# Sums by adding transfers a round ahead, and split float32r passes, in a two-layer encoder kernel

## The reference

```python
def rmsnorm(x, g):
    xf = xf * lax.rsqrt(jnp.mean(xf * xf, axis=-1, keepdims=True) + EPS)
    return (xf * g.astype(jnp.float32)).astype(x.dtype)

def gla(h, w_in, w_gate, b_gate, norm_w, w_o):
    proj = h @ w_in                       # q, k, v, g and the low-rank ga (16 columns)
    gk = jax.nn.log_sigmoid((ga @ w_gate + b_gate).astype(jnp.float32)) / B_GATE_NORM
    ...

def conv_ffn(h, w_up, conv_w, conv_b, w_down):
    u = h @ w_up
    gate, up = u[..., :D_FF], u[..., D_FF:]          # D_FF = 2816
    gp = jnp.pad(gate, ((0, 0), (CONV_W - 1, 0), (0, 0)))
    conv = conv_b + conv_w[0] * gp[:, 0:S]
    for i in range(1, CONV_W):
        conv = conv + conv_w[i] * gp[:, i:i + S]
    return (jax.nn.silu(conv) * up) @ w_down
```

## Time and profile before

| | |
|---|---|
| Median of 3 runs | 1114.54 us (1112.5 to 1115.76) |
| The profiled execution, its own time | 1112.34 us |
| Its span, first to last instruction | 1110.5 us |
| PE busy | 1078.2 us, 97% |
| DVE, ACT, POOL busy | 765.6, 490.3, 158.5 us |

### The profile page before, as it was taken

The page is one execution under the profiler, slowest core; times in us unless marked ns, Lnnn a source line. Parts: engine busy times, 40 slices in busy tenths (PEclk is TensorE's granted clock), DMA queues, the critical chain, the costliest instruction groups (busy, mean ns, idle before and its releaser), DMA issues.

```text
span 1110.5 us, 15662 instructions
## 1 busy us (share of the span) xinstructions
PE 1078.2 (97%) x5896; PEld 919.9 (83%) x5896; DVE 765.6 (69%) x1061; ACT 490.3 (44%) x755; POOL 158.5 (14%) x126
## 2 busy tenths in 40 slices
PE   6999999999999999989999999999999999999986
PEld 5888778888999888879788888878888999888886
DVE  4588666676986565998343656866676986565986
ACT  6366554443433334445652245444443433434442
POOL 6100030112000112012020221030112000112012
PEclk9999999999999999999999999999999999999998
DMA  6512032225242224241222211132225242224232
GB/s 193 157 59 74 22 112 95 94 94 169 88 146 100 95 95 154 73 141 64 76 77 95 81 52 58 59 112 95 94 94 171 86 155 92 95 94 155 72 117 88
DMA packets 39704, 112.38 MB, mean 101 GB/s; under 512 B 4769, under 2 KB 9537, under 8 KB 39650
## 3 DMA queue, kind: packets, MB, share of 16 engines
q1 hardware_dynamic: 34592, 106.45, 28.2%
q0 software_dynamic: 1152, 2.88, 1.6%
q10 hardware_dynamic: 3906, 2.31, 1.1%
HBM read 108.21 MB, written 2.88 MB: 100 GB/s over the span
## 4 chain that ended last, share of the span: by engine, by line
PE 43%; DVE 6%; ACT 2%; issue 1%; DMA 1%; POOL 0%; DVEq 0%; ACTq 0%; POOLq 0%
PE PS L444 33%; PE PS L497 6%; DVE WL L1260 1%; DVE DL_Z L1348 1%; PE PS L744 1%; ACT WH L863 1%; DVE DL_W L1348 1%; DVE X L1789 0%; PE PS L776 0%; PE PS L763 0%; DVE X L1393 0%; ACT SQ L893 0%; PE PS L747 0%; DVE DRAW_Z L1385 0%; DMA RAW<-w_down 0%
## 5 line engine op out<-in xcount | busy, mean ns | idle before, releaser
L444 PE MATMUL PS<-XH,WH 128*128 128x512 f32 x992 | 394.3, 397 | 8.7 <-DVE XL L1277 8.6
L444 PE MATMUL PS<-XH,WL 128*128 128x512 f32 x992 | 387.4, 391 | 0.0
L444 PE MATMUL PS<-XL,WH 128*128 128x512 f32 x992 | 387.1, 390 | 0.0
L444 PEld LDWEIGHTS PS<-XH,WH 128*128 128x128 f32 x992 | 186.9, 188 | 52.5 <-issue 11.4
L1260 DVE TENSOR_TENSOR WL<-WRAW,WH 128x1024 fp32r<-128x1024 f32 x137 | 193.4, 1412 | 51.5 <-ACT WH L863 50.8
L444 PEld LDWEIGHTS PS<-XL,WH 128*128 128x128 f32 x992 | 187.1, 189 | 39.2 <-issue 1.7
L444 PEld LDWEIGHTS PS<-XH,WL 128*128 128x128 f32 x992 | 186.8, 188 | 39.3
L863 ACT CAST WH<-WRAW 128x1024 fp32r<-128x1024 f32 x137 | 142.4, 1043 | 156.3 <-DMA WRAW<-w_up 99.5
L1834 POOL TENSOR_TENSOR CV<-CV,R 128x512 f32<-128x512 f32 x40 | 62.1, 1553 | 498.7 <-ACT CV L909 498.7
L497 PE MATMUL PS<-AH,DH_Z 128*128 128x256 f32 x352 | 99.5, 283 | 7.9 <-DVE X L1393 7.3
L1294 DVE TENSOR_TENSOR GS<-PS,R 128x512 f32<-128x512 f32 x44 | 30.4, 692 | 110.7 <-PE PS L444 110.5
(11 more groups left out here) (219 smaller groups left out, 1515.1 us busy)
## 6 DMA issues: line engine op xcount, KB each, us to landing
WRAW<-w_up SPq DMA_DIRECT2D x88, 512.0 KB, 3.2
WRAW<-w_bin SPq DMA_DIRECT2D x24, 512.0 KB, 3.2
DRAW_W<-w_down SPq DMA_DIRECT2D x24, 384.0 KB, 3.7
DRAW_W<-w_down SPq DMA_DIRECT2D x24, 320.0 KB, 3.4
WRAW<-w_qkv SPq DMA_DIRECT2D x11, 512.0 KB, 4.5
RAW<-w_down SPq DMA_DIRECT2D x12, 384.0 KB, 3.0
RAW<-w_down SPq DMA_DIRECT2D x12, 320.0 KB, 2.9
WRAW<-w_o SPq DMA_DIRECT2D x7, 512.0 KB, 3.2
```

The costliest lines, as they stand in the source:

```text
L444: last = mm(PS[:, bank], w[:, c:c + P], x[:, kb], start=start and n == 0 and w is wh and x is hi, stop=stop and n == len(kbs) - 1 and w is wl)
```

## The change

1. **Sums Z1 and Z3.** RAW21, RAW22, `sum_z1` and `sum_z3` go. Four buffers WSUM0 to WSUM3 hold them for rounds n+1 to n+3. SP loads W21 into each (`load_21`), POOL adds W22 or W11 by an adding transfer. Those for Z1 of round n+1 are issued when the last convolution of the chunk is done, those for Z3 of n+1 and both of n+2 when the last low part of the activations is done, ahead of the load of W11 for n+1; those of n+3 during round n+1.
2. **R onto the value half.** `values` multiplies the value unit's PSUM bank by R on DVE into RW, which frees the bank; `gated` multiplies RW by the SiLU. POOL's `gate` goes.
3. **Norm sums.** `SS` is split into SSH (ACT) and SSL (DVE), and `mean_square` runs two float32r passes with ones. For st 1 to 3 it comes one unit later, and for st 0 behind unit 2 instead of in its middle.
4. **Gate logits.** One float32r pass over 128 rows replaces the float32 product over 48: GAT and WGR hold high and low parts in four groups of rows. It comes one unit later (behind units 2 and 3).
5. **Order.** DVE's down rounds are reordered; the low parts of the next norm's input (`x_lo`) for tiles 0 to 5 move from three rounds into the last one.

```diff
-                sp.wait_ge(t_ready, FT * layer + F0[chunk] + 2 * PAIRS[chunk])
-                load_21(n + 1)
+                sp.wait_ge(conv_ready, FT * layer + F0[chunk] + 2 * PAIRS[chunk])
+                load_21(n + 1, "Z1")
                 sp.wait_ge(al_ready, AL_LAYER * layer + AL_COUNT[chunk] + 2 * PAIRS[chunk] + 1)
-                load_22(n + 1)
+                load_21(n + 1, "Z3")
+                load_21(n + 2, "Z1")
+                load_21(n + 2, "Z3")
...
-                if r in (1, 2):
+                if r == 1:
+                    sp.wait_ge(down_lo["Z1"], n + 1)
+                    load_21(n + 2, "Z1")
                     sp.wait_ge(down_lo["Z3"], n + 1)
-                    load_22(n + 1)
+                    load_21(n + 2, "Z3")
...
             def mean_square(st):
-                pe.wait_ge(ss_ready, KT_D * (st + 1))
-                mm(PS[:, B4], ONES[:], SS[:], start=True, stop=True).then_inc(ms_done, 1)
+                pe.wait_ge(ssl_ready, st + 1)
+                mm(PS[:, B4], ONESR[:], SSH[:], start=True, stop=False)
+                mm(PS[:, B4], ONESR[:], SSL[:], start=False, stop=True).then_inc(ms_done, 1)
...
-                mm(PS[:, B6 + t % 2], GAT[0:LO + RANK, t * P:(t + 1) * P], WG[0:LO + RANK, :],
-                   start=True, stop=True).then_inc(z_done, 1)
+                mm(PS[:, B6 + t % 2], GAT[:, t * P:(t + 1) * P], WGR[:], start=True, stop=True).then_inc(z_done, 1)
...
+            def values(layer, m, par):
+                dve.wait_ge(unit_done, UP[layer] + 2 * m + 2)
+                tt(RW[:, 3 * par:3 * par + 2], halves(PS[:, 2 * par + 1]), halves(R[:]), ALU.mult)\
+                    .then_inc(value_ready, 1)
...
+            def sum_z2(n):
+                dve.wait_ge(added["Z1", n % 2], 16 * (n // 2 + 1))
+                if n % 4:
+                    dve.wait_ge(down_done, COUNT[n - 1, "Z2"])
                 dve.wait_ge(plain["W11"], 16 * (n + 1))
...
             def down_rounds(n, st, next_unit):
                 take_z1(n)
-                take_w11(n)
                 weight_lo(n, "Z4")
                 weight_lo(n, "Z3")
                 take_w12(n)
-                sum_z1(n + 1)
                 take_z2(n)
-                sum_z3(n + 1)
                 sum_z2(n + 1)
                 weight_lo(n + 1, "Z1")
                 take_z4(n)
+                weight_lo(n, "W22")
+                weight_lo(n + 1, "W11")
                 sum_z4(n + 1)
-                weight_lo(n + 1, "W11")
-                weight_lo(n, "W22")
...
+                def add_quarter(n, name):
+                    onto, src = with_sum(n, name), "W22" if name == "Z1" else "W11"
+                    pool.wait_ge(first_half[name, n % 2], 16 * (n // 2 + 1))
+                    pool.dma_start(onto[:, 0:down_cols(n)], quarter(n, src), accum_op=ALU.add)\
+                        .then_inc(added[name, n % 2], 16)
...
+            link(tt(KS[:, 0], PS[:, B5], R[:], ALU.mult))
+            for first in GA_ROWS:
                 rows = slice(first, first + RANK)
-                last = tt(GAT[rows, :], PS[rows, B5], R[rows], ALU.mult)
-            last.then_inc(ga_ready, 1)
+                nc.vector.tensor_copy(GAT[rows, :], KS[rows, 0]).then_inc(gah_ready, 1)
+            dve.wait_ge(gah_ready, 4)
+            rows = slice(2 * LO, 2 * LO + RANK)
+            tt(GAT[rows, :], KS[rows, 0], GAT[rows, :].bitcast(F32), ALU.subtract).then_inc(ga_ready, 1)
```

More of the change, by code:

```diff
@@ L174, in trunk @@
         RW = place("RW", [P, 8, TH])
-        RAW21 = place("RAW21", [P, PAIRS[0] * P], at=place_at[0] - 32 * TH)
-        RAW22 = place("RAW22", [P, PAIRS[0] * P], at=place_at[0] - 20 * TH)
+        sums_at = place_at[0] - 32 * TH
         GS = place("GS", [P, 2, T + 2])
+        WSUM = [place(f"WSUM{i}", [P, PAIRS[0] * P], at=sums_at + 4 * i * PAIRS[0] * P) for i in range(4)]
+        assert sums_at + 16 * PAIRS[0] * P <= place_at[0]
         end_ffn = place_at[0]
@@ L264, in trunk @@
         t_ready, nt2_ready, gated_ready = sem("t_ready"), sem("nt2_ready"), sem("gated_ready")
[L265 to L268, removed]
+        plain = {name: sem(f"plain_{name}") for name in ("W11", "W12", "W22")}
+        first_half = {(name, r): sem(f"first_half_{name}_{r}") for name in ("Z1", "Z3") for r in range(2)}
+        added = {(name, r): sem(f"added_{name}_{r}") for name in ("Z1", "Z3") for r in range(2)}
+        summed = {name: sem(f"summed_{name}") for name in ("Z2", "Z4")}
         down_hi = {name: sem(f"down_hi_{name}") for name in PRODUCTS}
@@ L286, in quarter, with with_sum @@
             return (w_down0, w_down1)[chunk][layer, r, ("W11", "W12", "W21", "W22").index(name)]
-        def later(n):
-            return 3 * (n // 4) + n % 4
+        def with_sum(n, name):
+            if n % 4 == 0:
+                return DRAW["Z1"] if name == "Z1" else Z3RAW
+            return WSUM[((3, 1) if name == "Z1" else (0, 2))[n % 2 == 0]]
         def chunk_end(n):
@@ L325, in load_down, with load_21 @@
                 sp.dma_start(DRAW[name][:, 0:down_cols(n)], quarter(n, name)).then_inc(plain[name], 16)
[L327 to L333, removed]
+            def load_21(n, name):
+                sp.dma_start(with_sum(n, name)[:, 0:down_cols(n)], quarter(n, "W21"))\
+                    .then_inc(first_half[name, n % 2], 16)
             def load_up(layer, chunk):
@@ L477, in up_phase @@
                         if j == 3:
-                            pe.wait_ge(gated_ready, FT * layer + F0[1])
+                            pe.wait_ge(value_ready, FT * layer + F0[1])
                         unit(u0 + j, j, XH, XL)
-                    if chunk == 0 and j == 0:
+                    if chunk == 0 and j == 1:
                         mean_square(st)
@@ L572, in _ @@
             product(2, 2, XH, XL, range(0, 4), 0, stop=False)
-            pe.wait_ge(ones_set, 1)
+            product(2, 2, XH, XL, range(4, 8), 4, start=False).then_inc(unit_done, 1)
             mean_square(0)
-            product(2, 2, XH, XL, range(4, 8), 4, start=False).then_inc(unit_done, 1)
             unit(3, 3, XH, XL)
@@ L687, in _ @@
             last.then_inc(ga_done, 1)
-            mean_square(2)
             def gate_logits(t):
@@ L923, in weight_hi @@
             def weight_hi(n, name):
[L925 to L928, removed]
+                if name in ("Z1", "Z3"):
+                    act.wait_ge(added[name, n % 2], 16 * (n // 2 + 1))
                 elif name in ("Z2", "Z4"):
@@ L1334, in odd_lo, with last_lo @@
                 tt(parts(AL, kb, 2, 7), RW[:, 3:8], parts(AH, kb, 2, 7).bitcast(F32), ALU.subtract).then_inc(al_ready, 1)
[L1336 to L1340, removed]
-                tt(parts(AL, kb, 4, 7), RW[:, 5:8], parts(AH, kb, 4, 7).bitcast(F32), ALU.subtract).then_inc(al_ready, 1)
+            def last_lo(layer, chunk, kb, first, end):
+                dve.wait_ge(ah_ready, 2 * kb + (AL_LAYER * layer + AL_COUNT[chunk] + 2 + (first > 2)))
+                tt(parts(AL, kb, first, end), RW[:, first + 1:end + 1], parts(AH, kb, first, end).bitcast(F32), ALU.subtract)\
+                    .then_inc(al_ready, 1)
             def weight_lo(n, name):
@@ L1526, in down_rounds @@
                     lo_unit(next_unit)
+                if st is not None:
+                    x_lo(st, 4)
                 take_z3(m)
+                if st is not None:
+                    x_lo(st, 5)
                 if next_unit is not None:
```

196 lines of the change are left out of this document (104 added, 92 removed).

## The result

The changed kernel takes 1131.97 us (median of 4 runs, 1129.6 to 1134.98) against 1113.92 (4 runs) before, a ratio of 1.0163 [1.013, 1.0195]. The profiled execution took 1129.6 us with a span of 1127.8, 17.3 us more than the profiled one of before. The forecast was 1122, inside a range of 1105 to 1134: the direction held, the amount was more than twice the forecast one.

A forecast was written before the change was run, and what follows sets the result against it. PE, busy 97% of the span, was taken as the bound. Terms -8.5 + 6.0 + 7.7 + 3.0 - 1.7 + 1.1 + 0.5 = +8.1 us on 1112.34 gave 1120.4, moved by 2.2 to the median: 1122 us, range 1105 to 1134.

The forecast's parts named there:

- the order's 6.0: First rounds of the down chunks: W11 fourth in SP's queue makes them later, 6.0 us over four chunks, a lower bound.
- the addition's 7.7: First down rounds: adding transfers for Z1(n+1) share the engines and make W11 late by 7.7 us more.
- 0 to 15.4 for the additions: First down rounds: open range, in us, for W11's delay by the adding transfers for Z1(n+1) and Z3(n+1).
- The 1.84: Addend in PE's forecast wait ahead of Z1(n+1), six-block chunk: (890.4 + 1.84) - 888.4 = 3.8 us.
- that rival's 1133 us: Down chunks: both additions go ahead of W11, 7.7 us more and four slow stretches (+3); chance 0.20.
- The forecast 1.4 us ahead of W22(n): First down rounds: one of PE's longest waits, ahead of W22(n), four times, 1.4 us each.
- 3.0 for two slow stretches: Clock falls behind PE's waits ahead of Z1(n+1): two stretches taken of none to four, 1.5 us each.
- -8.5 + 0.5 = -8.0 us: Down chunks: 8.5 us gained from lighter DVE sums in five-block chunks, 0.5 lost to `x_lo` in layer 0's second chunk.
- 1 to 2 us a chunk: Second down rounds, if both additions precede W11: W22's weights behind W21 loads can be late too, total 1138 us.
- The 8.5 us of the takes: Five-block down chunks: fewer DVE sums shorten PE's waits for takes, restarts and slow clock: 5.9 us layer 0, 2.6 layer 1.
- Part 2: Up phases: one more DVE pass (0.69 us) for each of 44 tiles fits DVE's room; zero cost.
- The gates and the norm of st 2: Float32r passes for the norm sum and gate logits, less PE waits: net -1.7 us.

The follow-up runs named there:

- first experiment: Changed kernel with the two W21 loads for round n+2 issued behind W11 and W12 of round n+1: 1126.73 us, 1.010 to the kernel before.
- third: Changed kernel without the adding transfers of rounds n+1 to n+3, so those sums are left out: 1117.94 us, 1.0025 to the kernel before.
- fourth experiment: Changed kernel with W11 and W12 ahead of n+2's W21 loads, and n+3's Z3 W21 load behind W22, W11, W12: 1117.81 us, 1.0018 to before.
- the second: Changed kernel with DVE's takes of Z4 and Z3 and low parts of Z1(n+1), W22(n) ahead of Z2's sum: 1120.79 us, 1.0051 to before.
- the last version: Changed kernel with both SP load reorderings, DVE's first-round reordering and st 0's norm sum as before: 1109.20 us, 0.9957 to the kernel before.
- fifth experiment: Changed kernel with only the first norm's sum (st 0) as before, one float32 product: 1130.69 us, 1.0141 to the kernel before.
- the version with all three orders: Changed kernel with both SP load reorderings and DVE's first-round reordering, norm sums split: 1111.21 us, 0.9971 to the kernel before.

## Why the prediction came out as it did

**The first rounds: right in mechanism, somewhat too dear.** W11 is fourth in the queue, DVE idles for it ahead of the sum for Z2, PE waits longest ahead of Z1(n+1). The forecast had W11 make the first rounds later by 6.0 + 7.7 = 13.7 us. W11 took 7.5, 5.9, 6.4 and 5.4 us to land, where 6 to 9 were forecast. Z1(n+1) starts 4.1, 2.3, 3.1 and 1.7 us later in its chunk than before, 11.2 together. Without adding transfers it was 6.9, so the order's 6.0 measured 6.9 and the addition's 7.7 measured 4.4 (taken before rounding). The bounds (0 to 15.4 for the additions) held. The 1.84 in the forecast's sum for PE's wait ahead of Z1(n+1) stands in no row as a duration; 889.2 + 2.1 + 0.95 - 888.4 gives the same 3.8 us, and 3.6 and 2.5 were measured in the six-block chunks. The Trainium skill's rule ("DMA: Bandwidth & Descriptors", Queues, rings and completion order; round-robin between queues with work) would, by the prediction's reading, have put both additions ahead of W11; the measured 4.4 of 15.4 us speaks against that outcome. In layer 1's six-block chunk the second addition came too late to compete: POOL issued it at 895.51, when its own W21 had landed, its data began to move about 898.5, and W11 was there by 898.7. In layer 0's it overlapped W11 a little: the adding queue was at work again from 308.0, W11 landed at 309.9, and there the additions cost most, 1.9 us. The measured time lies close to that rival's 1133 us all the same; this is chance, its mechanism is not what the trace shows.

**W22(n): wrong in place, not in sum.** The forecast 1.4 us ahead of W22(n) did not come; none above 0.45 us. The slow stretch behind the Z1(n+1) wait covers it: PE is slow just then, and DVE catches up. Where the stretch is gone (first, third and fourth experiment), the wait is there, 0.94 to 1.05 us each time. At W22(n) the chunks are 4.5, 2.7, 3.1 and 2.0 us behind their schedule of before, 12.3 in all, against 13.7 + 3.0 for two slow stretches.

**The step that failed: what follows the first round.** From there to the ends of the chunks the forecast has -8.5 + 0.5 = -8.0 us. The trace has 16.5 - 12.3 = +4.2. Of the 12.2 between them, 9.2 are the waits ahead of Z3(n+1), which the prediction had only as an appendix to the rival with both additions, "1 to 2 us a chunk". It replayed DVE's list to the end of the first round, saw that `x_lo` and two sums leave the later rounds, and counted their waits as gone. It did not follow SP's queue into the second round. There `load_21(n + 2, "Z3")` waits for the low part of Z3(n+1), and W22(n+1) is behind it. Before, the same wait stood there, but the low part was early: in layer 1's six-block chunk it ended at 893.25, 17.5 us into the chunk, and what W22(n+1) waited for was its buffer, free when W22(n) ended at 893.74. Now W22(n) ends at 906.83, 3.8 us later in the chunk, and the low part at 908.32, 23.3 us into it, since DVE's list has it further back. So W22(n+1) leaves 5.5 us later: 3.8 are the late first round, handed on, and the rest is this wait. The fourth experiment takes the wait away, and there W22(n+1) goes out 0.2 us behind the end of W22(n). Late issue alone costs little: without adding transfers it goes out at nearly the same place (22.2 us into the chunk), lands after 3.9 us instead of 6.2, and PE loses 2.7 us in all four chunks. Late issue and slow landing together make the 9.2. The take that PE needs stands behind W22(n+1)'s low part on DVE.

**The clock: right kind, too few.** Two stretches at 1.5 were forecast in place of one; five came in the down phases, and a sixth in the start. In the down phases that is 5.8 us against 3.0 - 1.5. Of the four behind the Z1(n+1) waits, those of layer 0 end before W22(n) starts; of those of 902.1 and 1072.8, 1.6 and 0.7 us lie behind its start. By the 1.5 us for 3.4, these parts and the whole stretch of 499.3 are an estimated 2.5 of the remaining 3.0 of the 12.2. Two terms that the forecast took apart, the waits and the number of slow stretches, were coupled: a wait long enough to be forecast at 3 us is also one behind which the clock falls.

**The 8.5 us of the takes.** The long waits of the earlier trace rows did go: the sums of 1.70 and 1.65 us beside POOL are not in the trace after. In the kernel after, the waits ahead of Z1(n+1) and Z3(n+1) and the clock hide this: the five-block chunks are 4.8 us longer together. They are 2.3 us shorter than before in the fourth experiment, 4.7 in the second, with the takes moved, and 6.3 in the last. So the 8.5 us were not reached in any version.

**The rest.** Part 2 cost nothing: both later up phases take 108.82 us as before 108.81. The gates and the norm of st 2 gave 1.64 us, forecast 1.7. The start and the first up phase cost 2.4 us, forecast 1.1. In the start PE waits 2.97 us for the low part of unit 4, which the prediction had named, and a slow stretch lies behind it, which it had not; the fifth experiment takes 2.3 us back. In st 1 a wait for the low activations is 1.29 us, 0.59 before, and one of 0.83 for a weight's low part is new, 1.5 us together, where 0.75 was forecast. The `x_lo` of the last round cost 0.51 and 0.34 us, forecast 0.5.

The terms, forecast against measured: first rounds with their clock 16.7 and 12.3; rest of the down phases -8.0 and +4.2; start and st 1 +1.1 and +2.4; gates -1.7 and -1.6; sum +8.1 and +17.3.

**What stays open.** Why PE still loses 0.9 to 2.4 us a chunk in the second round of the last version; the order that would remove it was not tried. The trace shows that late issue is no longer the reason: in layer 1's six-block chunk W22(n+1) goes out 17.5 us into the chunk (18.15 before) and lands 6.6 us later (4.7 before). Why the matmuls start 0.118 us apart in some stretches and 0.113 in others. How much each of the two adding transfers of a round costs was not separated.

## What to carry to other kernels

When loads are moved ahead in an in-order queue, follow that queue through every later round, with the waits that stand in it: the second late weight cost here nearly as much as the first. Taking work from an engine gave nothing here until the transfers it waits for were in time; order the queue by when each weight is needed, and put prefetches for a later round last. And price a new wait of two and a half microseconds or more on TensorE with the clock behind it, 1.5 us more each time here.

## What the runs showed of the hardware

Around W11, adding and plain transfers hardly mixed in the kernel after. Windows of it, layer 0's five-block chunk, columns as in rows 2:

```profile
474.20:476.40 2.20, 1.76 (x15) 1.76 (x16) 2.19 (x5) 0.00 (x0) 0.00 (x0) 1.00 1.00 170
476.60:480.20 3.60, 3.43 (x31) 3.23 (x29) 0.42 (x1) 1.35 (x2) 1.75 (x2) 1.00 1.02 376
...
482.80:485.40 2.60, 2.60 (x13) 2.60 (x14) 2.60 (x6) 0.68 (x2) 0.00 (x0) 0.50 1.07 188
```

The rate is that of adding transfers alone (170, 188; the earlier trace rows have 187) or far above it (376), with the 16 engines full in all three. The profile's counts by queue (packets, MB, share of the 16 engines) in 474.20:476.00, then in 476.60:480.20, tell which kind it was. q0 carries the adding transfers: over the whole kernel it moved 2.88 MB before and 11.54 after, the bytes of 8 and of 32 of them.

```profile
q0 software_dynamic: 108, 0.27, 100.4%
q1 hardware_dynamic: 1, 0.00, 0.4%
...
q1 hardware_dynamic: 592, 1.35, 101.7%
```

So here the addition for Z1(n+1) goes first as a whole, though plain loads were issued from 473.55 on, and then the plain ones go alone. A plain load issued at 482.53 does not raise the rate of the third window either (q0 207 packets, q1 4). It is not always so: in the first experiment q0 and q1 move 0.16 and 0.23 MB in the same 1.5 us, from 476.5. The cost of the additions at Z1(n+1), the difference between 11.2 and 6.9 us, is uneven: 1.9, 1.0, 1.2 and 0.3 us, where one adding transfer alone takes 2.1 or 1.75. Why it is well below one in three of the four chunks, no run separates.

TensorE's granted clock fell to 0.50, the 1.2 GHz level, for 3.4 us (twice for 6.8) behind single short waits of a phase that is otherwise busy: behind every wait of 2.49 to 5.22 us in the kernel after and the seven experiments, and behind those of 1.9 to 2.3 us sometimes (2.28 at 1070.0 in the kernel after, 2.19 at 902.7 in the version with all three orders and 2.03 at 1088.6 in the one with the first norm's sum as before, but not 2.22 at 1084.2 in the kernel after, nor 2.29 at 478.1 in the one with the first norm's sum as before).
